# Context products of the second projection beside the first block's last norm, a carried expert order, and a prefilled expert sum

## The reference

```python
# first block, end
x = _ln_affine(DEEPNORM_ALPHA * x + (1.0 + m_l[2]) * yl, ln_g[i, 0], ln_b[i, 0])
hl = _modulate(x, m_l[3], m_l[4])
x = _ln_affine(DEEPNORM_ALPHA * x + (1.0 + m_l[5]) * _expert_choice_moe(hl, ...), ln_g[i, 1], ln_b[i, 1])
# second block
h_lat = modulate(rms_norm(x, norm1_g[l]), m_lat[0], m_lat[1])
h_ctx = modulate(rms_norm(ctx, norm1_g[l]), m_ctx[0], m_ctx[1])
pc = jnp.split(h_ctx @ w_in, cut, axis=-1)      # in hybrid_mixer; then depthwise
pl = jnp.split(h_lat @ w_in, cut, axis=-1)      # convolution over 5 and silu
x = x + m_lat[2][:, None] * mix_lat
h_lat = modulate(rms_norm(x, norm2_g[l]), m_lat[3], m_lat[4])
x = x + m_lat[5][:, None] * expert_choice_ffn(h_lat, router_w[l], ...)
return rms_norm(x, final_norm_g)
# both expert layers
xe = h[idx]; hid = silu(xe @ w_gate) * (xe @ w_up); ye = (hid @ w_down) * gate
zeros_like(h).at[idx].add(ye)
```

## Time and profile before

| | us |
|---|---|
| time, median of 3 (lowest, highest) | 4461.33 (4460.0, 4463.73) |
| the profiled execution's own time | 4461.8 |
| its span | 4460.1 |
| PE busy | 3867.7 (87% of the span) |
| DVE, ACT, POOL busy | 1509.0, 704.0, 459.3 |
| PE idle before the projection's transposes, waiting for the normed rows | 100.4 |

### The profile page before, as it was taken

How to read it: one execution, slowest core, us unless ns; L and a number is a source line. 1 busy time by engine, 2 the same in 40 slices (tenths; PEclk the granted TensorE clock), 3 DMA queues, 4 the chain that set the end, 5 groups by cost and what they waited for, 6 DMA issues and landing times. The chain is left out here.

```text
span 4460.1 us, 52698 instructions
## 1 busy us (share of the span) xinstructions
PE 3867.7 (87%) x22122; PEld 2172.1 (49%) x22122; DVE 1509.0 (34%) x2548; ACT 704.0 (16%) x1405; POOL 459.3 (10%) x513
## 2 busy tenths in 40 slices
PE   4999899969599999999999927999568998668994
PEld 2444488853244444444444414554447887234442
DVE  4655289945400000000000033440564555141003
ACT  1000022220100100010000012121253332011111
POOL 0000000002000000000000020000205554100110
PEclk8999999989799999999999968999789999888997
DMA  6576222232288888888888731111110001309994
GB/s 255 196 269 252 104 114 95 114 146 100 85 329 293 308 322 295 307 305 295 308 307 317 287 103 74 70 72 48 64 71 3 4 4 37 119 33 350 318 316 149
DMA packets 277343, 807.19 MB, mean 181 GB/s; under 512 B 9729, under 2 KB 17209, under 8 KB 261782
## 3 DMA queue, kind: packets, MB, share of 16 engines
q1 hardware_dynamic: 258010, 715.69, 43.3%
...
## 5 line engine op out<-in xcount | busy, mean ns | idle before, releaser
L1242 PE MATMUL banks<-moe_ring,moe_xeT 128*128 128x512 f32 x2560 | 1121.2, 594 | 4.5 <-ACT moe_xeT L1296 4.5
L1242 PEld LDWEIGHTS banks<-moe_ring,moe_xeT 128*128 128x128 f32 x2560 | 484.0, 191 | 596.0 <-issue 596.0
L1262 PE MATMUL banks<-moe_ring,moe_hidT 128*128 128x512 f32 x1280 | 565.7, 595 | 21.6 <-ACT moe_hidT L1303 21.6
L1332 DVE TENSOR_TENSOR moe_hid<-moe_silu,banks 128x512 f32<-128x512 f32 x80 | 55.0, 687 | 1293.1 <-PE banks L1242 1293.1
L1262 PEld LDWEIGHTS banks<-moe_ring,moe_hidT 128*128 128x128 f32 x1280 | 240.6, 190 | 320.1 <-issue 290.8
L1528 PE MATMUL banks<-hT,w_in_ring 128*128 128x512 f32 (+3 forms) x976 | 363.9, 536 | 4.3 <-ACT hT L1551 4.3
L434 PE MATMUL banks<-hT,w_in_ring 128*128 128x512 f32 x768 | 340.1, 597 | 3.4 <-ACT hT L456 3.4
L1528 PEld LDWEIGHTS banks<-hT,w_in_ring 128*128 128x128 f32 (+1 forms) x976 | 183.4, 188 | 184.6 <-issue 172.3
L968 PE MATMUL banks<-w_out,mix 128*128 128x512 f32 x512 | 231.0, 610 | 16.0 <-DMA w_out<-d_w_out 12.6
L1311 ACT ACTIVATE moe_silu<-banks 128x512 f32<-128x512 f32 x80 | 47.8, 598 | 1202.9 <-PE banks L1242 1202.9
L434 PEld LDWEIGHTS banks<-hT,w_in_ring 128*128 128x128 f32 x768 | 142.7, 190 | 192.5 <-issue 179.2
...
## 6 DMA issues: line engine op xcount, KB each, us to landing
moe_ring<-d_wg SPq DMA_DIRECT2D x80, 2048.0 KB, 12.7
moe_ring<-d_wu SPq DMA_DIRECT2D x80, 2048.0 KB, 17.5
moe_ring<-d_wd SPq DMA_DIRECT2D x80, 2048.0 KB, 8.0
x_normed<-d_ada_w SPq DMA_DIRECT2D x12, 2048.0 KB, 12.1
x_normed<-d_mod_w SPq DMA_DIRECT2D x8, 2048.0 KB, 15.1
d_taps<-dft SPq DMA_DIRECT2D x8, 2048.0 KB, 7.4
taps_in<-d_taps SPq DMA_DIRECT2D x8, 2048.0 KB, 9.4
w_in_ring<-d_hy_w_in SPq DMA_DIRECT2D x6, 2048.0 KB, 8.9
```

Source lines behind the costliest of these rows:

```text
L1242: last = nc.tensor.matmul(m.ps[:, 2 * kind + c, :], xeT[:, k, :], up(c, kind)[:, k, :], start=(k == 0), stop=(k == KT - 1))
L1262: last = nc.tensor.matmul(m.ps[:, Y_BANK + h, :], hidT[:, c, i * P:(i + 1) * P], down(c)[:, i, h * BANK:(h + 1) * BANK], start=(fc == 0 an ...
L1332: nc.vector.tensor_tensor(hid[:, j % 2, :], sg[:, j % 2, :], m.ps[:, 2 + j % 2, :], ALU.mult).then_inc(s.hid, 1)
```

## The change

- **out1, out2:** the zeros are gone. DVE's sum of residual and mixer output (in out1 the first norm's result) is stored to `acc` by POOL, tile by tile, when it is there.
- **moe1, moe2:** the transpose and the down product of an expert's last unit move into the next expert's first unit, as within an expert. SP's loads follow that order, the expert's result leaves one unit later (`leave`), three gathers run ahead in place of one, and POOL clears old semaphores in between. In the first block the results are scaled by 1/ALPHA, so that the table holds x + sum/ALPHA; the norm that follows has its epsilon divided by ALPHA squared.
- **fin1, fin2:** the table is loaded over the residual; L1392 is gone. fin1 is no stage any more.
- **min:** one stage does fin1's norm and the projection. SP loads the context rows, then latent tiles and the first two weight chunks mixed. DVE norms the context first; PE transposes it and runs all 17 context products, while DVE, ACT and POOL run the last norm of block one and the norm of block two, tile by tile. ACT does a step of these (`finished`) at two of three context products, and copies the product out. Half of the latent transposes stand behind context products 11 to 14, the other half behind the last. Then the 22 latent groups follow. Weights of the 17 context groups are loaded in 5 chunks of their own, so these columns come from memory twice. The context results are kept in `u2_ctx_padded` until the latent ones of their group are there. POOL stores the residual for out2 tile by tile.
- **Clearing:** `retire` is gone with its three blocks; POOL clears in moe1, moe2, min, the delta rule's preparation and out2.

```diff
-            pool.wait_ge(s.zero, 1)
-            for t in range(TT):
-                pool.dma_start(m.dram["acc"][t * P:(t + 1) * P, :], zeros[:]).then_inc(s.zeroed, 16)
+            for sem in spent:
+                pool.sem_clear(sem)
             if deep:
                 pool.wait_ge(s.pos, 2 * TT * 16)
                 for t in range(TT):
                     nc.gpsimd.tensor_tensor(m.X[:, t, :], m.X[:, t, :], xh[:, t, :], ALU.add).then_inc(s.sum, 1)
-            pool.wait_ge(s.zeroed, TT * 16)
+            for t in range(TT):
+                pool.wait_ge(s.summed, t + 1)
+                pool.dma_start(m.dram["acc"][t * P:(t + 1) * P, :], m.X[:, t, :]).then_inc(s.residual, 16)
+            pool.wait_ge(s.residual, TT * 16)
...
-                st.link(nc.vector.scalar_tensor_tensor(x, x, ALPHA if deep else 1.0, tmp[:].rearrange("p a b -> p (a b)"),
-                                                       ALU.mult, ALU.add))
+                both = tmp[:].rearrange("p a b -> p (a b)")
+                if deep:
+                    st.link(nc.vector.scalar_tensor_tensor(x, x, ALPHA, both, ALU.mult, ALU.add))
+                else:
+                    nc.vector.tensor_tensor(x, x, both, ALU.add).then_inc(s.summed, 1)
+                    v.wait_ge(s.summed, t + 1)
...
+            def load_down(weights, j, n):
+                fc, c = j % nf, j % 2
+                if not isinstance(n, int) or n >= 2:
+                    sp.wait_ge(s.d_mm, n - 1)
+                sp.dma_start(down(c), weights[:, fc * (EW // P):(fc + 1) * (EW // P), :]).then_inc(wd_in[c], 16)
...
+                    sp.dma_start(up(c, 1), pick(d_up, at[eu])[:, :, cols]).then_inc(wu_in[c], 16)
+                    if j:
+                        load_down(pick(d_down, at[(j - 1) // nf]), j - 1, n - 1)
+                    elif not first:
+                        load_down(pick(d_down, before), FU - 1, n - 1)
...
-            gather(0)
+            for e in range(3):
+                gather(e)
+            for sem in spent:
+                pool.sem_clear(sem)
             for e in range(E):
-                if e + 1 < E:
-                    gather(e + 1)
+                if e + 3 < E:
+                    gather(e + 3)
...
                     for fc in range(nf):
                         j = eu * nf + fc
-                        pe.wait_ge(s.hid, turn * FU + max(j - 1, 0))
+                        n = turn * FU + j
+                        if started or j:
+                            pe.wait_ge(s.hid, n - 1)
                         project(j, 0, wg_in, s.g_mm)
-                        if fc:
-                            turned(j - 1)
+                        if j:
+                            turned(j - 1, n - 1)
+                        elif started:
+                            turned(FU - 1, n - 1)
                         project(j, 1, wu_in, s.u_mm)
-                        if fc:
-                            back(j - 1)
-                    if eu == 0:
-                        rows(turn, 1)
-                    elif not final:
-                        rows(turn + 1, 0)
-                    turned(eu * nf + nf - 1)
-                    back(eu * nf + nf - 1)
+                        if fc == nf - 1:
+                            if eu == 0:
+                                rows(turn, 1)
+                            elif not final:
+                                rows(turn + 1, 0)
+                        if j:
+                            back(j - 1, n - 1, turn * EU + (j - 1) // nf, turn * (FU // 2 * 16) + ((j - 1) // 2 + 1) * 16)
+                        elif started:
+                            back(FU - 1, n - 1, turn * EU - 1, turn * (FU // 2 * 16))
+                if final:
+                    turned(FU - 1, E * nf - 1)
+                    back(FU - 1, E * nf - 1, E - 1, TURNS * (FU // 2 * 16))
...
+                        if fc == 0 and eu == 1:
+                            leave(0, settled(v, turn * EU), turn * FU + nf, turn * (EU * 16) - 16 if started else None)
+                        elif fc == 0 and started:
+                            leave(1, settled(v, turn * EU - 1), turn * FU, turn * (EU * 16) - 16)
+                if final:
+                    leave(1, E - 1, E * nf, (TURNS - 1) * (EU * 16))
...
-                st.link(nc.vector.scalar_tensor_tensor(x, x, ALPHA if deep else 1.0, acc[:, t, :], ALU.mult, ALU.add))
...
+            for t in range(TT):
+                sp.dma_start(m.X[:, t, :], m.dram["acc"][t * P:(t + 1) * P, :]).then_inc(arrived[t], 16)
+                if t in (1, 3):
+                    weights(t // 2)
+            for q in range(2, N_CHUNKS):
+                weights(q)
+            sp.wait_ge(s.p_mm, chunk_done(N_CHUNKS - 2))
...
+            pool.wait_ge(s.params, 32)
+            for t in range(TT):
+                pool.wait_ge(s.scaled, t + 1)
+                nc.gpsimd.tensor_tensor(m.X[:, t, :], m.X[:, t, :], ln[:, 1, :], ALU.add).then_inc(s.done, 1)
+                pool.wait_ge(s.done, t + 1)
+                pool.dma_start(m.dram["xres"][:, t, :], m.X[:, t, :]).then_inc(s.kept, 16)
...
+            pe.wait_ge(s.ctx_xh, CT)
+            for k in range(KT):
+                for i in range(CT):
+                    last = nc.tensor.transpose(m.ps[:, k, i * P:(i + 1) * P], ctx[:, i, k * P:(k + 1) * P], m.ident[:])
+                last.then_inc(s.tr_mm, 1)
+            pe.wait_ge(s.hT, LATE)
+            for i in range(CTX_UNITS):
+                q = i // PER_CHUNK
+                if i % PER_CHUNK == 0:
+                    pe.wait_ge(w_in[q % 2], (q // 2 + 1) * 16)
+                product(i, q, (i % PER_CHUNK) * P, P if i < CONV_T else SMALL, T, CTX)
+                if TURN_FROM <= i < TURN_FROM + 4:
+                    for n in range(2 * (i - TURN_FROM), 2 * (i - TURN_FROM) + 2):
+                        turned(n)
+            for n in range(KT, 2 * KT):
+                turned(n)
+            pe.wait_ge(s.hT, 3 * KT)
+            for i in range(LAT_UNITS):
                 c = i // PER_CHUNK
+                q = CTX_CHUNKS_W + min(c, LAT_CHUNKS_W - 1)
                 if i % PER_CHUNK == 0:
-                    pe.wait_ge(w_in[c % 2], (c // 2 + 1) * 16)
-                width = P if i < PROJ_T else SMALL
-                at = (i % PER_CHUNK) * P
-                for j, (first, n) in enumerate(parts_of(i)):
-                    g = parts_before(i) + j
-                    if g >= 6:
-                        pe.wait_ge(s.p_read, g - 5)
-                    for k in range(KT):
-                        last = nc.tensor.matmul(m.ps[0:width, g % 6, 0:n], ring[:, c % 2, k, at:at + width],
-                                                hT[:, k, first:first + n], start=(k == 0), stop=(k == KT - 1))
-                    last.then_inc(s.p_mm, 1)
+                    pe.wait_ge(w_in[q % 2], (q // 2 + 1) * 16)
+                for j, (first, n) in enumerate(PARTS):
+                    product(group_of(i, j), q, (i % PER_CHUNK) * P, P if i < PROJ_T else SMALL, first, n)
...
+            def finished(t):
+                if t < TT:
+                    act.wait_ge(s.var, t + 1)
+                    nc.scalar.activation(frstd[:, t:t + 1], frstd[:, t:t + 1], ACT.Sqrt).then_inc(s.std, 1)
+                    nc.scalar.activation(m.X[:, t, :], m.X[:, t, :], ACT.Identity, bias=fmv[:, t, 0:1]).then_inc(s.centred, 1)
+                if 2 <= t < TT + 2:
+                    act.wait_ge(s.var2, t - 1)
+                    nc.scalar.activation(rstd[:, t - 2:t - 1], rstd[:, t - 2:t - 1], ACT.Sqrt).then_inc(s.std2, 1)
+                if t >= 3:
+                    act.wait_ge(s.inv_std, t - 2)
+                    nc.scalar.activation(xh[:, t - 3, :], m.X[:, t - 3, :], ACT.Copy, scale=rstd[:, t - 3:t - 2]).then_inc(s.xh, 1)
...
+            for i in range(CTX_UNITS):
+                if i % 3 != 2 and i - i // 3 < TT + 3:
+                    finished(i - i // 3)
+                act.wait_ge(s.p_mm, i + 1)
+                if i < CONV_T:
+                    nc.scalar.copy(uc[:, i, PAD:PAD + CTX], m.ps[:, i % 6, 0:CTX]).then_inc(s.p_read, 1)
+                else:
+                    nc.scalar.copy(small[0:32, T:TA], m.ps[0:32, i % 6, 0:CTX]).then_inc(s.small, 1)
+                    nc.scalar.copy(small[32:SMALL, T:TA], m.ps[32:SMALL, i % 6, 0:CTX]).then_inc(s.p_read, 1)
+                if TURN_FROM <= i < TURN_FROM + 4:
+                    for n in range(2 * (i - TURN_FROM), 2 * (i - TURN_FROM) + 2):
+                        turned(n)
...
+            for t in range(TT + 3):
+                if t < TT:
+                    arrive(t)
+                if 1 <= t < TT + 1:
+                    scale(t - 1)
+                if 2 <= t < TT + 2:
+                    length(t - 2)
+                if t >= 3:
+                    v.wait_ge(s.std2, t - 2)
+                    nc.vector.reciprocal(rstd[:, t - 3:t - 2], rstd[:, t - 3:t - 2]).then_inc(s.inv_std, 1)
...
-def retire(nc, m):
-
```

(13 more changed lines are left out.)

333 lines of the change are left out of this document (201 added, 132 removed).

## The result

| | before | after |
|---|---|---|
| time, median (lowest, highest) in us | 4462.53 (4460.0, 4464.53) | 4315.91 (4314.97, 4316.51) |
| profiled execution, its span in us | 4461.8, 4460.1 | 4315.75, 4314.1 |
| PE busy in us (share of the span) | 3867.7 (87%) | 3852.5 (89%) |

The ratio is 0.9671, with a 95% interval of 0.9658 to 0.9685: 146 us less. The forecast was 4320, with a range of 4303 to 4352. Unless a unit is named, numbers in the text are us.

What follows compares the result with a forecast made beforehand. TensorE, busy in 87% of the span, was taken to set the end almost everywhere, so only its idle time could be won. Gains 77.4 + 4.0 + 30.5 + 10.9 + 9 + 9.8 = 141.6 off 4461.8 gave 4320 us, range 4303 to 4352.

Steps and rivals of the forecast that it cites:

- The sum: Whole kernel: all predicted gains together, 141.6 us off the profiled execution's 4461.8, giving 4320.2.
- Term 1: Block one's last norm and the projection in one stage: norms hidden behind context products, gain 77.4 us, bounds 72 and 82.
- The cover: Merged norm and projection stage: norms end some 10 us before TensorE needs the last tile.
- Term 2: z product: its 4.03 us wait for weights goes, as the new load threshold is passed earlier; gain 4.0 us.
- Term 3: Experts of both blocks: carried order removes breaks between experts; gain 13.2 + 17.3 = 30.5 us, lower bound 20.4.
- Term 4: Second and third clearing blocks: POOL clears beside other engines' work instead; gain 4.0 and 6.9, together 10.9 us.
- term 5: out1 and out2: without stores of zeros, output weights are waited for less; 8 us in out2, 1 in out1.
- Term 6: Last norm, at the kernel's end: eight DVE sum instructions of 1.22 us go; gain 9.8 us.
- TensorE waits for ScalarE: Rival, merged stage: ScalarE serves norms and copies in one order, so TensorE stands; 4340 us, chance 0.13.
- No wait for weights in the experts: Denies a rival: experts are bound by weights, so the carried expert order gains 0; 4350 us, chance 0.07.
- TensorE did not stay slow: Denies a rival: the 17 context products run at the lower clock throughout, twice 58.7 us; 4379, chance 0.05.
- The queue did not become slower: Denies a rival: in-order SP issue delays expert gate loads, each of 80 units waits; 4510 at 2 us, chance 0.02.

Runs made afterwards that it cites:

- the early stage: Changed kernel, but the first block's experts no longer wait for the last scatter to land; the projection stage starts at once and waits later: 4318.27 us.

## Why the prediction was right, and where it was not

- **The sum (141.6)** is 4.4 short of the 146.0 between the two traces, and misses cancel in it. Above the forecast lie 2.4 us at the start, 2.8 between experts and z product and 3.0 in the z product; below it 2.1 in the second block's experts and 2.0 in the delta rule. The 2.4 and the 2.0 are the spread shown above, and that they and the others offset each other is luck. The own range was also mis-added: the better ends of terms 1 and 5 give 4311 or 4312, not 4305. The result lies in either.
- **Term 1 (77.4).** Right in mechanism and size. Terms 1 and 2 made 84.2 together for 81.4. The start came 17.6 us behind the stage's first load (16.7 forecast), the transposes cost 10.5 (11.7), and the slow start of 3 us that the earlier trace rows show, which the forecast had kept, did not come: the first twelve products ran at a granted clock of 1.00. That was not certain. In nine traces with these products seven show 41.71 us for them, the run with the zeros 43.35 and the early stage 43.93. Undoing terms 1 and 2 gave 67.5 of the 67 expected.
- **The cover** was mis-sized: 5 to 7 us, not 10. I had counted VectorE at 5.6 us a tile, measured 5.91, and looked at the last tile: its scaling ended 4.9 us before TensorE took it (2662.88 + 1.14 against 2668.91). What gave way first was ScalarE's copy of the first transposes. It changed nothing, but one more instruction per tile cost 2.8 us in the stage. The reading that the old loop meets the lock "once in eight tiles" is VectorE's side alone; GpSimd's additions took 3.2 us beside the sums (L1392) and 2.34 for the last two tiles. The third of eight, in the kernel before:

```profile
2630.51 3.26 POOL L1371 TENSOR_TENSOR x_block<-x_block,fin_ln 128x1024 f32<-128x1024 f32 x1 [1.21 <-DVE x_block L1410]
```

- **Term 2 (4.0).** The gain came, by another cause. The step "the new threshold is passed two latent groups earlier" is not what removes the wait: the order that ends with latent products hides 3.4 of the 4.0 by itself.
- **What no term had: 3.0 us of slower z product** behind the old wait. The rows before showed it (44.55 us for 128 instructions); I read only the wait. The 3.4 us at the start look alike (the first 16 output products took 9.99 us before and 7.13 now), but there other runs with the same program took 8.8 to 9.2, so no gain of this change is shown.
- **Term 3 (30.5).** The first block gave 13.15 of 13.2. In the second, 15.2 of 17.3: under "what is late next" I named the hidden rows and the result, and missed that the first expert has no carried product behind its rows (2.55 us).
- **Term 4 (10.9) and term 5 (9).** Term 4 gave 3.6 and 6.1 for 4.0 and 6.9. Of term 5, out2 gained 8.8 for 8 (2.8 of the first wait, 6.0 behind it), and lost 6.8 in the stage and 8.0 in time when the zeros were put back; the 1 us of out1 can't be told from the spread. **Term 6 (9.8)** was 10.0.
- **The rivals.** Among the 17 context products TensorE waits for ScalarE not once, though the runs with extra instructions show how near that was. No wait for weights in the experts, with a DMA share of 0.92 in the second block; a granted clock of 1.00 in all context products, so TensorE did not stay slow there. The swinging clock of the Trainium skill (TensorE: Matmul & The Clock Gate, "A second HAM failure mode: psum-queue depth-cycling") did not show in these products. The queue did not become slower but faster. Weights of the experts on the page, KB and us to landing, where 12.7 and 17.5 stood before:

```profile
moe_ring<-d_wg SPq DMA_DIRECT2D x80, 2048.0 KB, 8.4
moe_ring<-d_wu SPq DMA_DIRECT2D x80, 2048.0 KB, 8.3
```

- The -2.0 us in the delta rule (510.6 for 508.6) are within the 508.1 to 511.7 of the other runs, whose program there is the same.

The Trainium skill (SBUF — State Buffer, "Who interferes with whom") has the lock between an instruction of VectorE with two inputs in the buffer and a GpSimd one that reads it. The trace agrees: beside the addition the moments (one input) took 1.28 us as ever, and L1743, with two, 0.98 instead of 0.22.
